# A gate's weights move ahead of the last two expert slabs, and its products run by channel chunks

## The reference, cut to what matters

```
h = rms_norm(x, norm_mix) ; z = h @ w_in            # q, k, v, cu, cg, ga, gb
x = x + (sigmoid(ga) * attention(q, k, v) @ w_attn_out + sigmoid(gb) * conv(cu, cg) @ w_conv_out ...) @ w_out
h2 = rms_norm(x, norm_ffn)
x = x + moe(h2)                                     # 32 experts of width 512, two per token
                                                    # hb = silu(xb @ w_gate[e]) * (xb @ w_up[e]) ; hb @ w_down[e]
g_ple = sigmoid(rms_norm(x, norm_ple) @ w_ple_gate) # [256, 1024] @ [1024, 1024]
x = x + g_ple * (p @ w_ple_proj)                    # p is [256, 256]
```

## Time and profile before

| what | value |
|---|---|
| runs | 1923.93, 1925.07, 1927.21 us (median 1925.07) |
| profiled execution | 1927.43 us; first to last instruction 1925.7 us |
| PE busy | 1654.3 us, 86% |
| DVE busy / ACT busy | 733.5 us / 365.8 us |
| transfers | 564.73 MB, mean 293 GB/s over the span |
| the two seams (layer 0 to layer 1, layer 1 to the second block) | about 616 to 690 us, about 1278 to 1345 us |

### The profile page before, as it was taken

One profiled execution on the slowest core, in us unless ns is written; L12 is line 12 of the kernel. 1 busy time (PEld: TensorE's weight loads), 2 busy tenths in 40 slices (PEclk: granted clock), 3 DMA queues, 4 the chain that ended last, 5 costly groups with the idle time before them and its releaser, 6 DMA issues. The chain is left out here.

```text
span 1925.7 us, 19591 instructions
## 1 busy us (share of the span) xinstructions
PE 1654.3 (86%) x8204; PEld 946.4 (49%) x8204; DVE 733.5 (38%) x1263; ACT 365.8 (19%) x796; POOL 0.2 (0%) x4
## 2 busy tenths in 40 slices
PE   9999985666766999999765766769999999999999
PEld 8546532222222784475221322228888865474444
DVE  5984210001100479632110101005638457745554
ACT  2342200000000223412000000003044234312200
POOL 0000000000000000000000000000000000000000
PEclk9999998788878999999887878889999999999999
DMA  8447899999999853479999999993544523344442
GB/s 359 174 146 328 342 425 431 431 431 430 430 427 430 335 224 131 178 324 382 434 426 430 432 432 428 431 425 148 198 154 154 208 88 131 131 151 155 150 168 97
DMA packets 31628, 564.73 MB, mean 293 GB/s; under 512 B 3633, under 2 KB 4145, under 8 KB 5553
## 3 DMA queue, kind: packets, MB, share of 16 engines
q1 hardware_dynamic: 31536, 563.42, 71.2%
HBM read 562.36 MB, written 1.05 MB: 293 GB/s over the span
## 5 line engine op out<-in xcount | busy, mean ns | idle before, releaser
L1633 PE MATMUL ps<-ring,hB 128*32 128x512 f32 x1024 | 150.6, 741 | 100.8 <-DMA ring<-in_stream 100.8
L1633 PE MATMUL ps<-l_extra,hB 128*32 128x512 f32 x768 | 120.2, 770 | 57.4 <-DMA l_extra<-in_stream 55.5
L1633 PEld LDWEIGHTS ps<-ring,hB 128*32 128x32 f32 x1024 | 40.2, 132 | 195.8 <-issue 194.9
L1645 PE MATMUL ps<-ring,hB 128*32 128x512 f32 x512 | 83.4, 808 | 57.4 <-DMA ring<-in_stream 57.4
L734 PE MATMUL ps<-late,ring 128*128 128x256 f32 x576 | 125.3, 379 | 0.0
L734 PEld LDWEIGHTS ps<-late,ring 128*128 128x128 f32 x576 | 109.4, 190 | 14.9
L1743 DVE COPY hB<-ps 128x512 f32<-128x512 f32 x16 | 11.1, 692 | 277.3 <-PE ps L1645 277.3
L1741 DVE TENSOR_TENSOR hB<-ps,hB 128x512 f32<-128x512 f32 x16 | 11.1, 692 | 274.1 <-ACT hB L1716 274.1
L2105 PE MATMUL ps<-late,ring 128*128 128x256 f32 x512 | 111.5, 379 | 0.0
L2105 PEld LDWEIGHTS ps<-late,ring 128*128 128x128 f32 x512 | 97.3, 190 | 14.9 <-issue 1.9
L1299 DVE SCALAR_TENSOR_TENSOR l_extra<-l_extra,lpar 128x255 f32<-128x255 f32 (+14 forms) x240 | 101.7, 465 | 5.9 <-ACT l_extra L1155 2.6
(11 more groups left out here) (462 smaller groups left out, 2353.6 us busy)
## 6 DMA issues: line engine op xcount, KB each, us to landing
ring<-in_stream SPq DMA_DIRECT2D x80, 2048.0 KB, 7.8
ring<-in_stream SPq DMA_DIRECT2D x40, 4096.0 KB, 52.2
l_extra<-in_stream SPq DMA_DIRECT2D x26, 4096.0 KB, 52.6
l_extra<-in_stream SPq DMA_DIRECT2D x28, 2048.0 KB, 38.7
late<-in_stream SPq DMA_DIRECT2D x16, 2048.0 KB, 48.8
ring<-in_stream SPq DMA_DIRECT2D x2, 2024.0 KB, 8.2
ring<-in_stream SPq DMA_DIRECT2D x2, 1664.0 KB, 6.7
ring<-in_stream SPq DMA_DIRECT2D x2, 1536.0 KB, 18.8
```

What stands on the lines that cost most here:

```text
L1633: mm = nc.tensor.matmul(out[js, :], x_slots[:, c, js], w[:, 0, j * D + at:j * D + at + FF], start=(c == 0), stop=(c == DC - 1))
L1645: mm = nc.tensor.matmul(y_banks[half][js, :], hidT[:, f, js], w[:, 0, j * D + half * BANK:j * D + (half + 1) * BANK], start=(f == 0), stop ...
```

## The change

1. Down slabs hold, instead of a chunk f of hidden channels with all 1024 output columns, a quarter c of the output columns (256) with all hidden channels. `down(c)` makes 16 products of 256 columns where `down(f)` made eight of 512. The first half of y is then whole after two slabs.
2. In the stream the gate's two slabs stand ahead of the last two down slabs of a layer (`GATE_FROM`), in the slots `pairs[0]` and `pairs[1]`.
3. In the last quad each quarter of y is copied by ACT as it is done (`y_part`), combined, added and scaled. The gate's products run by input chunks: chunks 0 to 3 while the last two down slabs come, 4 and 5 behind down slab 3, the mean of squares, then 6 and 7. Partial sums stay open in banks 0, 1, 4, 5 and 2; so ACT copies the ple product from its banks to SBUF (`keep_ple`), and the pieces read it there.
4. The next layer's q runs chunk by chunk for its first three outputs, then the mean of squares, then the fourth output.
5. Ahead of the second block `keep_busy` waits for the mean's bank instead of the gate's second piece.

```diff
+GATE_FROM = MOE_SLABS - FC // 2
...
-        return self.first[layer, "moe"] + m + (m >= MOE_SLABS - FC)
+        return self.first[layer, "moe"] + m + (m >= MOE_SLABS - FC) + 2 * (m >= GATE_FROM)
...
         for m in range(single, MOE_SLABS):
+            if m == GATE_FROM:
+                for n in range(2):
+                    s.add((l, "ple_gate"), [pairs[n]], P, DC, BANK, m0 + MOE_SLABS + 1 + n)
             s.add((l, "moe"), [place[(m + 1) % CYCLE]], P, 1, SLAB, m0 + m)
-        tail = ring if l < DEPTH - 1 else range(3, RING)
-        for _ in range(2):
-            s.add((l, "ple_gate"), tail, P, DC, BANK)
...
-        dn = np.asarray(a["w_exp_down"][l]).reshape(QUADS, QUAD, FC, P, D).transpose(0, 2, 3, 1, 4)
+        dn = np.asarray(a["w_exp_down"][l]).reshape(QUADS, QUAD, FC, P, FC, T).transpose(0, 4, 3, 1, 2, 5).reshape(QUADS, FC, P, QUAD, D)
...
-        for stage, bs in dict(ple=(0, 1, 4, 5), mean_ple=(7,), ple_gate=(2, 3, 6, 7, 2),
+        for stage, bs in dict(ple=(0, 1, 4, 5), mean_ple=(3,), ple_gate=(0, 1, 4, 5, 2),
...
-    def ple_tensor(self, pe, claim, layer):
+    def ple_tensor(self, pe, claim, layer, down, combine):
...
+        def gate_part(b, ks):
+            w = store.wait(pe, i + b // 2)
+            pe.wait_ge(self.scaled["ple"], ks[-1] + 1)
+            for m in range(2):
...
+                for k in ks:
+                    mm = self.nc.tensor.matmul(out[:, at:at + T], w[:, k, c * P:(c + 1) * P], self.hA[:, k, :],
+                                               start=(k == 0 and at == 0), stop=(k == DC - 1 and (m == 1 or b == 3)))
...
+        gate_part(0, range(2))
+        gate_part(1, range(2))
+        gate_part(0, range(2, 4))
+        gate_part(1, range(2, 4))
+        gate_part(2, range(4))
+        down(2)
+        pe.wait_ge(self.y_part, 2)
+        gate_part(3, range(2))
+        combine(2)
+        down(3)
+        gate_part(3, range(2, 4))
+        gate_part(0, range(4, 6))
+        combine(3)
+        for b in range(1, 3):
+            gate_part(b, range(4, 6))
         self.mean_square(pe, claim, "ple")
...
+        for b in range(3):
+            gate_part(b, range(6, 8))
+            if b == 1:
+                store.free(i, self.filled["ple_gate"], 2)
+        gate_part(3, range(4, 8))
         store.free(i + 1, self.filled["ple_gate"], 5)
...
     def ple_scalar(self, act, step, then_norm):
+        last = QUADS - SPLIT - 1
         for b in range(4):
-            act.wait_ge(self.part_added, 4 * (QUADS - SPLIT - 1) + b + 1)
+            if b >= 2:
+                act.wait_ge(self.slab_used, last * QUAD_SLABS + DC + b + 1)
+                self.nc.scalar.copy(self.y_last[:, b * T:(b + 1) * T], self.ps[2 + b // 2][:, b % 2 * T:(b % 2 + 1) * T])\
+                    .then_inc(self.y_part if b == 2 else self.y_left, 1)
+            act.wait_ge(self.part_added, 4 * last + b + 1)
             self.square_bank("ple", b)
...
-        for b in range(5):
-            if b < 4:
+        for half in range(2):
+            for b in (2 * half, 2 * half + 1):
                 self.add_part(dve, added + b)
-            if b:
-                dve.wait_ge(self.part_added, added + b)
-                self.scale_by_gain(layer, "ple", range(2 * b - 2, 2 * b))
-        for b in range(4):
-            self.sum_bank(dve, step, "ple", b)
+                dve.wait_ge(self.part_added, added + b + 1)
+                self.scale_by_gain(layer, "ple", range(2 * b, 2 * b + 2))
+            if half:
+                dve.sem_inc(self.y_right, 1)
+            for b in (2 * half, 2 * half + 1):
+                self.sum_bank(dve, step, "ple", b)
...
-        out = claim("q", 0)
-        for m in range(2):
-            for k in range(DC):
-                if m == 0:
-                    pe.wait_ge(self.scaled["mix"], k + 1)
-                    if k == (0 if layer else DC // 2):
-                        store.wait(pe, i)
-                mm = nc.tensor.matmul(out[:, m * T:(m + 1) * T], w[:, k, m * P:(m + 1) * P], self.hB[:, k, :], start=(k == 0), stop=(k == DC - 1))
-        mm.then_inc(filled["q"], 1)
+        outs = [claim("q", b) for b in range(2)]
+        for k in range(DC):
+            pe.wait_ge(self.scaled["mix"], k + 1)
+            if k == (0 if layer else DC // 2):
+                store.wait(pe, i)
+            for m in range(3):
+                mm = nc.tensor.matmul(outs[m // 2][:, m % 2 * T:(m % 2 + 1) * T], w[:, k, m * P:(m + 1) * P], self.hB[:, k, :],
+                                      start=(k == 0 and m != 1), stop=(k == DC - 1 and m == 1))
...
         self.mean_square(pe, claim, "mix")
-        self.fill_bank(pe, claim, "q", 1, w, 1, self.hB, DC)
+        for k in range(DC):
+            mm = nc.tensor.matmul(outs[1][:, T:2 * T], w[:, k, 3 * P:4 * P], self.hB[:, k, :], start=False, stop=(k == DC - 1))
+        mm.then_inc(filled["q"], 1)
...
-        def down(q, n, f):
-            i = store.slabs.expert(layer, q * QUAD_SLABS + DC + f)
+        def down(q, n, c):
+            i = store.slabs.expert(layer, q * QUAD_SLABS + DC + c)
             w = store.wait(pe, i)
-            for half in range(2):
+            out = y_banks[c // 2][:, c % 2 * T:(c % 2 + 1) * T]
+            for f in range(FC):
                 for j in range(QUAD):
                     js = slice(SLOTS * j, SLOTS * (j + 1))
...
+                    mm = nc.tensor.matmul(out[js, :], hidT[:, f, js], w[:, 0, j * D + f * T:j * D + (f + 1) * T],
                                           start=(f == 0), stop=(f == FC - 1))
...
-            for f in range(FC):
-                down(q, n, f)
-                if q == QUADS - 1 and f < FC - 1:
-                    if f == 1:
-                        pe.wait_ge(self.put_copied, n + 1)
-                    self.fill_bank(pe, claim, "ple", f + 1, w, f + 1, pT, PLE // P)
-                    if f == FC - 2:
+            for c in range(FC // 2 if q == QUADS - 1 else FC):
+                down(q, n, c)
+                if q == QUADS - 1:
+                    self.fill_bank(pe, claim, "ple", 2 * c + 1, w, 2 * c + 1, pT, PLE // P)
+                    combine_last(c)
+                    if c == 0:
+                        self.fill_bank(pe, claim, "ple", 2, w, 2, pT, PLE // P)
+                    else:
                         store.free(i, self.filled["ple"], 4)
-        combine(n)
...
+    def keep_ple(self, act, b):
+
+        act.wait_ge(self.filled["ple"], b + 1)
+        self.nc.scalar.copy(flat(self.ple_kept[:, pair(b), :]), self.bank("ple", b)[:]).then_inc(self.emptied["ple"], 1)
...
                     if not head:
-                        pe.wait_ge(self.emptied["ple_gate"], 2)
+                        pe.wait_ge(self.emptied["mean_ple"], 1)
                         self.keep_busy(self.ps[3], self.const[:, C_UPTO:C_UPTO + T], 7)
```

More of the change, by code:

```diff
@@ L630, in __init__ @@
         self.stat, self.rstd = (store.late[:, 3072 + T * i:3072 + T * i + T] for i in range(2))
-        self.sq = dict(ple=self.hB, mix=extra[:, 1, 0:2048].rearrange(three, c=DC), ffn=work[:, 0:2048].rearrange(three, c=DC))
+        self.ple_kept = extra[:, 3, 0:2048].rearrange(three, c=DC)
+        self.sq = dict(ple=extra[:, 4, 0:2048].rearrange(three, c=DC), mix=extra[:, 1, 0:2048].rearrange(three, c=DC), ffn=work[:, 0:2048].rearrange(three, c=DC))
         self.hg = dict(ple=self.hA, mix=self.hB, ffn=self.hA)
@@ L639, in __init__ @@
         self.y_slots = flat_b[:, DC * P:2 * DC * P]
+        self.y_last = flat_b[:, 0:DC * P]
         self.hid_slots = self.y_slots[:, 0:FF]
@@ L698, in claim @@
                 s, n = last_in[b]
-                pe.wait_ge(self.emptied[s], n + 2 if n == 3 and s == "ple" else n + 1)
+                pe.wait_ge(self.emptied[s], n + 1)
             last_in[b] = (stage, i)
@@ L1610, in turn_put, with combine_pair @@
             mm.then_inc(self.put_filled, 1)
+        def combine_pair(n, b, y):
+            k = 4 * n + b
+            if k >= 2:
+                pe.wait_ge(self.part_added, k - 1)
+            for m in range(2):
+                c = 2 * b + m
+                mm = nc.tensor.matmul(part_banks[b % 2][:, m * T:(m + 1) * T], y[:, c * P:(c + 1) * P], put, start=True, stop=True)
+            mm.then_inc(self.part_filled, 1)
         def combine(n):
@@ L1617, in combine, with combine_last @@
                     pe.wait_ge(self.y_right, n + 1)
-                k = 4 * n + b
-                if k >= 2:
-                    pe.wait_ge(self.part_added, k - 1)
-                for m in range(2):
-                    c = 2 * b + m
-                    mm = nc.tensor.matmul(part_banks[b % 2][:, m * T:(m + 1) * T], y_slots[:, c * P:(c + 1) * P], put,
-                                          start=True, stop=True)
-                mm.then_inc(self.part_filled, 1)
+                combine_pair(n, b, y_slots)
+        def combine_last(b):
+            pe.wait_ge(self.put_copied, n + 1)
+            if b < 3:
+                pe.wait_ge(self.y_part, b + 1)
+            else:
```

(19 more changed lines are left out.)

55 lines of the change are left out of this document (28 added, 27 removed).

## The result

The changed kernel takes 1929.71 us (median of 12 runs, 1926.23 to 1930.88), the kernel before 1925.16 beside it (12 runs, 1921.84 to 1929.08). The ratio, taken from runs side by side, is 1.002 with a 95% interval of 1.0011 to 1.0029, which is 2.1 to 5.6 us: slower, by a fifth of a percent. The forecast was 1927.2, +2.1. The profiled execution took 1929.96, its span is 1928.2.

What follows compares the result with a forecast made beforehand. Transfers pace the expert stage; PE sets the pace of both seams, DVE close behind. Seam 1 -3.1, seam 2 +3.3 and the clock +2.0 sum to +2.2 us, 1927.2 or so on the median; range 1922.5 to 1934.5.

Steps and rivals of the forecast that it cites:

- case A: The sum of both seams and the clock: +2.2 us, 1927.2 or so, own range 1924.5 to 1930; chance 0.58.
- Down slabs: 32 passes of 256 columns take 1.86 us a slab, as the 16 of 512 did; upper bound +0.9 a slab.
- Rival B: Weight loads stand open on eight down slabs in the two seams, 0.9 us each: +7.1, 1934.3; chance 0.17.
- Transfers: The gate's two slabs and the last two down slabs swap landings, from 631.3 to 646.0 us, without harm.
- Seam 1: From layer 0's last down slabs to the next layer's cu: cu at 681.9 instead of 685.03, -3.1 us.
- Seam 2: Last layer's down slabs to the second block, which waits for DVE's last scaling: 1336.6 against 1333.26, +3.3 us.
- Rival D: DVE keeps up with PE's 1.73 us a bank behind the mean: together -7.2 us, 1917.9; chance 0.10.
- Clock: Second block's start, behind 7.3 us of idle PE: the low clock costs +2.0 us, range 0 to 3.6.
- Rival C: The clock holds behind seam 2's gap and the first q's gain stays: -0.7 us, 1924.4; chance 0.15.
- First q: Kernel start: q chunk by chunk would save 0.9 us, but PE later waits for ACT's probabilities; taken as 0.

Runs made afterwards that it cites:

- e4: The kernel before with only the down slabs laid out by output columns (32 passes of 256 columns a slab): 1922.57 us, ratio 0.9997.
- e6: The kernel before with only the transfers' order changed, the gate's two slabs ahead of the last two down slabs: 1946.03 us, ratio 1.0105.
- e2: The changed kernel with DVE's pieces interleaved, the next piece's multiplication by the root ahead of the rest of this one: 1924.15 us, ratio 0.9997.
- e1: The changed kernel with 20 instead of 7 idle products behind the gate in seam 2: 1927.40 us, ratio 1.0017.
- e3: The changed kernel with the old orders back in seam 2, the down layout kept: 1922.57 us, ratio 0.9992 to the kernel before.
- e7: The changed kernel with one gate slab behind each of the last two down slabs, 28 gate products before the mean: 1921.00 us, ratio 0.9980.
- e11: e7 run once more, beside e9 and e10: 1921.87 us, ratio 0.9986 to the kernel before.
- e10: e8 with gate banks 0 and 1 finished before bank 2's remaining products behind the mean: 1921.81 us, ratio 0.9988.
- e5: The changed kernel with the last combining product and the mean of squares moved ahead of two groups of four gate products: 1928.06 us, ratio 1.0017.
- e9: e5 with gate banks 0 and 1 finished before bank 2's remaining products behind the mean: 1925.80 us, ratio 1.0009.
- e8: The changed kernel with the edits of e5 and e2 together: 1923.55 us, ratio 0.9992 to the kernel before.

## Why the forecast held, and where it was off

The time lies at the upper end of case A's own range (1924.5 to 1930), and the parts of its mechanism are those of the traces: the seams' terms follow one by one.

**Down slabs.** 1.86 us for 32 passes of 256 columns, as taken from the earlier trace rows, in the changed kernel and in e4. Rival B is refuted. The Trainium skill (TensorE: Matmul & The Clock Gate, "The mechanism" of Part 3) says that weight loads overlap running matmuls only where the row groups differ. The trace does not agree: all rows were in use, and the 32 loads of 32 columns lay within the 1.86 us, which is no more than the 16 passes with 16 loads took.

**Transfers.** In time: G0, D2 and D3 landed within a microsecond of the forecast. e6 shows the price if PE's order did not follow: 10 us a seam.

**Seam 1.** -2.9 us (60.88 against 63.77), forecast -3.1; the mean at +36.64 instead of +36.2; the wait in q 0.53 instead of 1.1.

**Seam 2.** +3.0 us, forecast +3.3; pieces 3.48 to 3.50 us apart, the halves 2.15 and 2.2. e2, which changes DVE's order alone, gives the three microseconds back, so the mechanism is shown and not only argued. Rival D needed pieces of 2.5 us; even interleaved they take 2.69.

**Clock.** +2.7 us (9.65 against 6.98), forecast +2.0 from a gap of 6.79 in the expert stage: a third more than forecast. Rival C (the clock holds) did not occur in the changed kernel's profiled execution. This term is the least certain of the sum, because it is a draw of one execution: behind 3.43 us it was nothing once and 1.7 once, and e1, whose profile has none of it, is by its ratio hardly faster.

**First q.** Nothing, as forecast, though in the changed kernel's execution for another reason (q began late). e2 shows the forecast's: cu 0.93 us earlier, and the products at 92.31 no earlier than before (92.29).

The seams' sum is -2.9 + 3.0 + 2.7 = +2.8, forecast +2.2; measured are +3.9 by the ratio and +4.55 by the medians. On the trace's own clock the account goes otherwise: the changed kernel's D0 started 2.18 us late in seam 1, so that cu gained only 0.71 us (684.32 against 685.03) and seam 2's D0 1.42. The lateness goes with a stretch at the low clock over layer 0's transposes, as PE's timeline shows, first of before, then of the changed kernel:

```profile
205.58 1.94 PE L1107 MATMUL ps<-const,late 128*128 128x128 f32 x16
```

```profile
206.01 3.65 PE L1144 MATMUL ps<-const,late 128*128 128x128 f32 x16
```

e4, the only other profile with a late D0, is also the only other one with such a stretch (the same 16 products take 3.37 us). That the one causes the other is likely but not shown. At the end of the second block's first 32 passes the changed kernel is 4.22 us behind (1346.10 against 1341.88), and it ends 2.5 behind, because the profiled execution of before had 1.7 us of low clock later on (a mean of 0.98 between 1500 and 1600, 1.00 in the changed kernel). So that the sum comes out so near is in part luck: draws of the clock of 1.7 us each, in layer 0, behind the gap and in the second block, are as large as its terms, and the runs of one kernel spread over up to 7 us. **The step that was left out of the sum** is that the new order starts from D0 and not from a landing, so a late D0 counts in full, where before D3's landing absorbed it (e4). It is rare in the profiles: of the ten kernels in which PE follows the new order, D0 of seam 1 started at 623.44 in the changed one and at 621.6 to 622.2 in the other nine.

What stays open: in every kernel in which PE follows the new order the measured ratio is worse than what its seams give against before, by 0.6 to 3.2 us. For e1, e2 and e3 the seams sum to +0.2, -3.8 and -4.2 us, the ratios are +3.3, -0.6 and -1.5, with some 1.7 us to either side; for e7 and e11 they sum to -5.1, measured are -3.9 and -2.7; for e10 it is -3.1 and -2.3. Two reasons lie in the measure. e4 keeps the old order, and its seams sum to -3.3 against -0.6 measured, so counting from D0 flatters it. And the one profiled execution of before took 1927.43 us, 2.3 above the median of its twelve runs. A late D0 in most executions would be a third reason, but the profiles speak against it. How much each explains is not shown.

## What to carry to other kernels

Work moved ahead of a reduction is hidden only if what hangs on the reduction has other cover: count what is left behind the reduction and hold it against the other engine's own pace. Here 20 gate products (8.6 us) faced 15 us of DVE work; where q stood behind them it paid, where a barrier did it did not. The best split of those tried moved less: 28 of the 64 products stood before the mean instead of 44, against 16 in the old order (e7). The order within the moved part must follow the consumer (e5 against e9). An idle gap ahead of PE-bound work costs its length and can cost once more in the clock behind it.

## What the runs showed of the hardware

- 32 column-tiled passes of 128 rows by 32 columns with 256 moving columns keep the rate of 16 with 512: 1.86 us for either. Each has its own weight load, 32 of them in the same time (changed kernel and e4).
- The length of the gap alone did not tell what it cost. Behind 6.39 and 5.88 us of gap the first 32 passes took 9.65 and 9.75 us, behind 4.65 and 2.46 8.67, behind 3.43 once 6.99 (e2) and once 8.67 (e8), behind 0.89 always 6.98 or 6.99. Each is one execution.
- Idle products brought the clock over such a gap at no cost to the block's start (54.97 against 54.85 us behind D0): 40 passes in place of 14 kept it at 1.00 in e1's profile. The ratio of e1 gained only 0.0003.
